# Per-head sums of squares as two products of the rounded 32-bit type

## The reference, cut to what matters

```python
def _rmsnorm(x, g):
    xf = x.astype(jnp.float32)
    r = lax.rsqrt(jnp.mean(xf * xf, axis=-1, keepdims=True) + EPS)
    return (xf * r).astype(x.dtype) * g

def _shared_kv(h, g, w_kv, f_bias, g_k):
    N, L, _ = h.shape
    k, v, f = jnp.split(_rmsnorm(h, g) @ w_kv, [D_ATTN, 2 * D_ATTN], axis=-1)
    k = _rmsnorm(k.reshape(N, L, N_HEADS, HEAD_DIM), g_k)
    ...
def _fox_layer(x, attend, g, w_in, g_q, w_out):
    q, z = jnp.split(_rmsnorm(x, g) @ w_in, 2, axis=-1)
    q = _rmsnorm(q.reshape(N, L, N_HEADS, HEAD_DIM), g_q)
    o = attend(q).reshape(N, L, D_ATTN)
    return x + (o * jax.nn.silu(z)) @ w_out
```

## Time and profile before

| what | us |
|---|---|
| median of 3 executions | 965.12 (964.96 to 965.85) |
| the profiled execution | 964.84 |
| its span, first to last instruction | 963.0 |
| PE busy | 931.7 (97% of the span) |
| DVE busy | 492.6 (51%) |
| ACT busy | 383.9 (40%) |
| POOL busy | 163.0 (17%) |
| granted TensorE clock | full (1.00) |

### The profile page before, as it was taken

One profiled execution on the slowest core, in us unless ns is written; L12 is line 12 of the kernel. 1 busy time (PEld: TensorE's weight loads), 2 busy tenths in 40 slices (PEclk: granted clock), 3 DMA queues, 4 the chain that ended last, 5 costly groups with the idle time before them and its releaser, 6 DMA issues.

```text
span 963.0 us, 23705 instructions
## 1 busy us (share of the span) xinstructions
PE 931.7 (97%) x8516; PEld 800.4 (83%) x8516; DVE 492.6 (51%) x1133; ACT 383.9 (40%) x728; POOL 163.0 (17%) x111
## 2 busy tenths in 40 slices
PE   4999999999999999999999999999999999999998
PEld 4999999999998997868778778688687787776898
DVE  5775555556345334463554554544545545535632
ACT  5333333322135443553543544535444445345210
POOL 2233333332030221102002012011020020000000
PEclk9999999999999999999999999999999999999999
DMA  7233322224343516889799799798996997987412
GB/s 235 67 88 87 87 70 83 81 72 118 127 153 115 174 57 201 284 292 351 239 367 332 238 385 302 264 380 257 329 348 233 371 328 240 383 297 254 142 44 99
DMA packets 133333, 206.41 MB, mean 214 GB/s; under 512 B 8847, under 2 KB 91456, under 8 KB 133170
## 3 DMA queue, kind: packets, MB, share of 16 engines
q1 hardware_dynamic: 121602, 198.35, 60.8%
q10 hardware_dynamic: 11168, 5.51, 2.1%
q0 software_dynamic: 528, 2.10, 0.8%
HBM read 195.29 MB, written 10.63 MB: 214 GB/s over the span
## 4 chain that ended last, share of the span: by engine, by line
PE 80%; DMA 6%; DVE 4%; ACT 3%; SPq 3%; issue 3%; ACTq 0%; DVEq 0%
PE psum L1221 41%; PE psum L1201 16%; PE psum L1270 9%; PE psum L1404 7%; DMA page_ring<-in_cache_k 4%; PE psum L1519 2%; ACT sample_scores L707 2%; SPq L375 2%; SPq L377 1%; DMA w_raw<-in_a_w_out 1%; PE psum L1447 1%; DMA residual<-in_x_prompt 1%; PE psum L1319 1%; PE psum L1427 1%; DMA page_ring<-in_cache_v 1%
## 5 line engine op out<-in xcount | busy, mean ns | idle before, releaser
L1221 PE MATMUL psum<-xn_high,w_high 128*128 128x256 f32 (+1 forms) x992 | 236.4, 317 | 2.6 <-DVE w_low L832 2.6
L1221 PE MATMUL psum<-xn_low,w_high 128*128 128x256 f32 (+1 forms) x992 | 215.8, 296 | 0.0
L1221 PE MATMUL psum<-xn_high,w_low 128*128 128x256 f32 (+1 forms) x992 | 215.6, 296 | 0.0
L1221 PEld LDWEIGHTS psum<-xn_high,w_high 128*128 128x128 f32 x992 | 163.1, 191 | 16.8 <-issue 13.3
L1221 PEld LDWEIGHTS psum<-xn_high,w_low 128*128 128x128 f32 x992 | 168.3, 190 | 0.0
L1221 PEld LDWEIGHTS psum<-xn_low,w_high 128*128 128x128 f32 x992 | 168.2, 190 | 0.0
L1201 PE MATMUL psum<-constants,page_ring 128*128 128x128 f32 x1024 | 136.9, 276 | 3.7 <-DMA page_ring<-in_cache_k 2.4
L1201 PEld LDWEIGHTS psum<-constants,page_ring 128*128 128x128 f32 x1024 | 114.0, 140 | 29.8 <-issue 27.6
L501 POOL TENSOR_TENSOR w_raw<-w_raw,gains 128x1024 f32<-128x1024 f32 x32 | 61.5, 1925 | 338.4 <-DMA w_raw<-in_b_w_in 217.6
L832 DVE TENSOR_TENSOR w_low<-w_raw,w_high 128x1024 fp32r<-128x1024 f32 x32 | 58.2, 1819 | 67.0 <-ACT w_high L565 67.0
L1009 DVE COPY k_turned_odd<-psum 128x512 f32<-128x512 f32 x64 | 44.1, 690 | 93.5 <-PE psum L1201 93.5
(11 more groups left out here) (236 smaller groups left out, 1467.8 us busy)
## 6 DMA issues: line engine op xcount, KB each, us to landing
page_ring<-in_cache_k SPq DMA_DIRECT2D x128, 512.0 KB, 5.8
page_ring<-in_cache_v SPq DMA_DIRECT2D x128, 512.0 KB, 5.2
w_raw<-in_a_w_in SPq DMA_DIRECT2D x30, 512.0 KB, 4.0
suffix<-suffix_scratch SPq DMA_DIRECT2D x32, 256.0 KB, 4.8
w_raw<-in_b_w_in SPq DMA_DIRECT2D x16, 512.0 KB, 6.8
w_raw<-in_kv_w SPq DMA_DIRECT2D x16, 512.0 KB, 6.2
w_raw<-in_a_w_out SPq DMA_DIRECT2D x4, 1024.0 KB, 5.1
f_broad<-f_scratch SPq DMA_DIRECT2D x8, 512.0 KB, 6.3
```

The source lines that it names most:

```text
L1221: mm = pe.matmul(PS[:, bank + h, 0:c.stop - c.start], w[:, k, :], x[:, k, c], start=(k == 0 and n == 0), stop=(k == KT - 1 and n == 2))
```

## The change

The squares are split like all other operands. DVE copies `SQ` to a rounded high part `SQH` (which lies in the last slab of the tile `gated_low`) and overwrites `SQ` with the rest, `SQL` (tile `squares_low`). PE multiplies both with a rounded copy of the ones matrix, `ONER`, and adds the two products in PSUM. In the query stage the sum moves from behind piece k = 2 to behind k = 3, and the split stands first in DVE's `query`, ahead of `low_b`. In the head stage the split stands at k = 6 behind the two gain instructions and ahead of the copy of T1; PE's sum stays behind the turns of k = 9.

```diff
         dve.wait_ge(s_fp, 1)
+        dve.tensor_copy(ONER[:, :], CT[:, C_ONESB:C_ONESB + P]).then_inc(s_one, 1)
...
+        def split_squares(high, done, n):
+
+            dve.tensor_copy(SQH, SQ[:, :]).then_inc(high, 1)
+            dve.wait_ge(high, n)
+            dve.tensor_tensor(SQL[:, :], SQ[:, :], SQH.bitcast(F32), ALU.subtract).then_inc(done, 1)
+
         def query(m, s):
+            dve.wait_ge(q_sq, m + 1)
+            split_squares(q_hi, q_sp, m + 1)
             low_b(m + 2, s)
...
                     dve.tensor_scalar(KN_T[:, SEQ:TOK], sa, gk, None, ALU.mult).then_inc(b_ddve, 1)
+                    dve.wait_ge(b_dact, 2 * i + 1)
+                    split_squares(b_hi, b_sp, i + 1)
                 turned1(KTS[k // 2 % 2][:, 4:8, c:c + PAGE],
...
+        def sum_squares():
+            for n, x in enumerate((SQH, SQL)):
+                pe.matmul(PS[:, OS, 0:NS], ONER[:, :], x[:, SEQ:TOK], start=(n == 0), stop=(n == 1))
+                mm = pe.matmul(PS[:, OP, :], ONER[:, :], x[:, 0:SEQ], start=(n == 0), stop=(n == 1))
+            return mm
...
-                if k == 2:
+                if k == 3:
                     if weights:
                         pe.wait_ge(s_fneg, 1)
-                    pe.wait_ge(q_sq, m)
+                        pe.wait_ge(s_one, 1)
+                    pe.wait_ge(q_sp, m)
...
         query(KT - 1, 1)
-        pe.wait_ge(q_sq, KT)
+        pe.wait_ge(q_sp, KT)
         pe.wait_ge(q_rr, KT - 1)
         q_sum()
...
-                    pe.wait_ge(b_dact, 2 * i + 1)
+                    pe.wait_ge(b_sp, i + 1)
```

More of the change, by code:

```diff
@@ L170, in build @@
     WFL = place("wf_low", [P, KT, H], F32R)
+    ONER = place("ones_blocks", [P, P], F32R, over=at["wf_high"])
+    SQL = place("squares_low", [P, TOK], F32R, over=at["squares"])
+    SQH = GL[:, KT - 1, :]
     PTAB = place("page_row", [1, NB * NPG], I32)
@@ L242, in build @@
     s_ck = sem("f_new_loaded")
+    s_one, q_hi, q_sp, b_hi, b_sp = (
+        sem("ones_ready"), sem("q_squares_high"), sem("q_squares_split"), sem("head_squares_high"),
+        sem("head_squares_split"))
     q_sq, q_ss, q_ln, q_rr, q_out = sem("q_squares"), sem("q_summed"), sem("q_ln"), sem("q_rsqrt"), sem("q_ready")
@@ L1315, in _ @@
         norm_turn(4, 1)
+        def sum_squares():
[3 more added lines that the diff above has]
+            return mm
         def q_sum():
-            pe.matmul(PS[:, OS, 0:NS], CT[:, C_ONESB:C_ONESB + P], SQ[:, SEQ:TOK], start=True, stop=True)
-            pe.matmul(PS[:, OP, :], CT[:, C_ONESB:C_ONESB + P], SQ[:, 0:SEQ], start=True, stop=True).then_inc(q_ss, 1)
+            sum_squares().then_inc(q_ss, 1)
         def query(m, s, weights=None):
@@ L1421, in heads @@
                 if k == 9:
-                    pe.wait_ge(b_dact, 2 * i + 1)
+                    pe.wait_ge(b_sp, i + 1)
                     pe.wait_ge(b_gf, i)
                     pe.wait_ge(b_sot, i)
-                    pe.matmul(PS[:, OS, 0:NS], CT[:, C_ONESB:C_ONESB + P], SQ[:, SEQ:TOK], start=True, stop=True)
-                    pe.matmul(PS[:, OP, :], CT[:, C_ONESB:C_ONESB + P], SQ[:, 0:SEQ], start=True, stop=True).then_inc(b_ss, 1)
+                    sum_squares().then_inc(b_ss, 1)
                 if k < 6:
```

## The result

| | before | after |
|---|---|---|
| median, us (lowest to highest, runs) | 965.04 (962.05 to 965.85, 4) | 978.15 (975.66 to 980.91, 4) |
| ratio, 95% interval | | 1.014 (1.0117 to 1.0163) |
| profiled execution: time, span | 964.84, 963.0 | 975.66, 973.8 |

The account below looks back on a forecast made before the run. PE's own stream was taken as the bound. 964.84 + 8.8 (eight head steps) + 0.7 (POOL in the first step) + 1.3 (query stage) = 975.6, stated as 975.4 us; range 970.5 to 980.5.

Parts of the forecast that it names:

- PE is the path, and DVE's order sets its waits: Head stage, k = 6: T1's copy waits behind DVE's split, stalling PE 1.5 us plus 0.05 in each of eight steps.
- The split: On DVE: a copy of 0.50 us and a subtraction of 0.76, with 0.03 between, 1.3 us (1.3 to 1.55).
- The sum on PE: Each of 16 sums of squares falls from 1.07 to 0.62 us, saving 0.45 (0.29 to 0.54).
- First head step: First head: the usual +1.1 us and +0.7 because the split waits for POOL's weight scaling; +1.8.
- Last stretch: Last gain to the end of the span, holding the eighth stall: +1.1 us.
- Query stage: From DVE's `f_raw` to the first head's gain: start, shorter periods, POOL and end together +1.3 us (-0.9 to +3.5).
- Collisions: Query stage: POOL's scaling meets the split in four queries, stalling PE 0.4, 0.8, 0.8 and 0.1 us, +2.1.
- Clean period: Query stage: one query without POOL in the way takes 7.1 us instead of 7.48, -0.38.
- PE doesn't need T1 early: Head stage: T1's copy has slack for the split, so only savings stay and the total is 962.5 us; 5%.
- waits for pages absorb it: Head stage: PE's waits for cached pages take up the stall, at most 4.6 us, total 971; 7%.
- POOL blocks more: POOL holds up the split in all queries and several head steps, total 980 us; 15%.
- 64 columns as dear as the full type: PE's sums: a rounded 64-column product costs as much as the full 32-bit one, 2.6 us more, total 978.0; 12%.

Follow-up runs that it names:

- x8_split_k7: Changed kernel with the head stage's split moved on DVE from k = 6 to the end of k = 7; 965.60 us, ratio 1.0005.
- x10_two_more_casts: Changed kernel with the old query stage and two more copies of the squares ahead of the heads' split; 988.48 us, ratio 1.0259.
- x4_pe_only: Changed kernel, but ACT writes rounded squares, no split, both products read them (low part left out), sum behind k = 2; 958.91 us, ratio 0.9940.
- x5_pe_only_cut: Changed kernel with ACT writing rounded squares, no split, low part left out, and sums cut 256 and 320 columns; 957.20 us, ratio 0.9902.
- x2_query_only: Changed kernel with the head stage of the kernel before, the query stage as changed; 966.81 us, ratio 1.0029.
- x6_small_pool: Changed kernel with POOL's scalings behind the fourth shrunk to eight elements, waits and signals kept; 976.11 us, ratio 1.0115.
- x3_late_split: Changed kernel with the head stage's split moved on DVE from k = 6 to the end of k = 8; 968.40 us, ratio 1.0049.
- x9_last_full: Changed kernel with the last query's sum in the full 32-bit type and unsplit; 977.73 us, ratio 1.0126.
- x7_best: Changed kernel with the old query stage, the heads' split at the end of k = 7 and their sums cut 256 and 320; 962.05 us, ratio 0.9969.

## Why the prediction was right, and where its sizes were off

- **PE is the path, and DVE's order sets its waits**: right. Eight waits at the named place. At the one worked out the fifth turn is 1.52 late against a forecast of 1.5, and 1.57 with the slower turn behind it against 1.55. `x8_split_k7` takes the wait away and 12.5 us with it; `x10_two_more_casts` lengthens it one for one.
- **The split**: 0.46 + 0.76, starts 0.50 apart, against 0.50 + 0.76. Right. The 0.36 us for the copy by the page's table (the Trainium skill, VectorE: DVE Perf Modes, errata cycle table), which the forecast had set aside, is 0.10 too short here. The same section says so itself: this row under-predicts, and the fixed part measures about 150 cycles, by which an estimate is (150 + 288) / 0.96 = 0.46 us, as in the trace.
- **The sum on PE**: mis-sized. I took 0.08 us for a rounded product of 64 columns; the sum came out at 0.68 instead of 0.62 and the saving at 0.40 instead of 0.45. Where the time goes is shown by `x4_pe_only` and `x5_pe_only_cut`: the even cut takes 0.53, so all that lies above it comes from the cut with 64 columns. In a head the stall was 1.57 for 1.55 and the saving 0.40 for 0.45, which makes up the 0.08 by which an ordinary step grew more than forecast (1.18 for 1.1).
- **First head step**: +2.3 for +1.8. Up to the piece behind the sum it went as forecast: the fifth turn is 2.11 late, 0.6 of it POOL's (PE waits 1.94 where the others are 1.36; forecast 0.7), and behind the sum PE is 1.77 late against the forecast's 1.8. The other 0.55 comes at the end of the step, at the value and key pages, which the forecast had put at nothing either way: PE waits 0.94 for a value page where it was 0.70 (the rows under the stages), and the turns of a key page 2 us later lose another 0.3. Why these pages come later stays open.
- **Last stretch**: +1.6 for +1.1. Its wait is longer than in an ordinary step (1.50 for 1.36), and PE waits 0.65 for a value page where it was 0.35. The stretch also moves by itself: in `x2_query_only`, with the heads of the kernel before, it takes 124.32 where that kernel took 124.69.
- **Query stage**: +2.8 for +1.3, and here the terms were wrong by different amounts. Collisions: 2.0 measured (`x6_small_pool`), 2.1 forecast; the agreement is luck, as the next point says. Clean period: 7.27 in the mean measured, 7.1 forecast; five times 0.17 is 0.85. Part of that is the sum's 0.06, since the chain to `q_out` runs through it. The 0.7 that is left is TensorE's clock behind the last query's wait: 6.94 in the changed kernel and 6.24 in two others with the same wait at a full clock, and 77.10 for 76.37 in two kernels that differ only in their heads. No term of the forecast held it.
- I had followed POOL's collisions as if they would fade (0.4, 0.8, 0.8, 0.1). They don't: the four periods are 0.4, 0.5, 0.5 and 0.5 longer than the clean one. POOL starts 3.9 to 4.0 us behind the end of `low_b`, which stands behind the split, so a delayed split delays the next scaling by as much, and the two meet at the same phase again, 7.8 us later each time.
- **Rivals.** *PE doesn't need T1 early* and *waits for pages absorb it* fell: the waits for pages are 4.2 us in all after 4.6. *POOL blocks more* fell in the heads for the place that the change chose, but `x3_late_split` shows how near it was: two pages later, four of eight splits are hit. *64 columns as dear as the full type* lies between: 0.68 is between my 0.62 and its 0.78.
- The net: heads +11.0 measured and +9.5 forecast, query stage +2.8 and +1.3, in all 13.8 and 10.8 (the stages' -2.9 at the start aside). The terms of the forecast itself add up to 975.6, and no term stands for the 0.2 by which it says 975.4. Of the 3.0 between, 0.6 lies in the ordinary head steps, 0.5 in the first, 0.4 in the last, 0.9 in the clean query periods and 0.7 in the clock.

## What to carry to other kernels

Before work goes to an engine that is half idle, look up what stands behind the place where it is put in that engine's queue, and which buffer the bound engine wants next: here the same two instructions cost 1.5 us per head behind page 6 and nothing that PE waited for behind page 7. Then look for long instructions of the neighbour that shares SBUF with it, at the new time of day, not the old one. And cut rounded products evenly: 256 and 320 columns took 0.27 us a set where 64 and 512 took 0.34. Cut evenly, the sum would save 0.54 us and not 0.40.

## What the hardware showed that I had not expected

- **DVE can be held for nearly a whole instruction of POOL.** A cast of 0.46 us took 1.90 and 1.97, and a subtraction of 0.76 took 2.33, under one scaling of 1.90, which itself took up to 2.14 in the changed kernel. The last is new beside the earlier trace rows: at 336.60 to 337.10 the cast, the scaling and the subtraction began within 0.5 us, the cast took its 0.46, and the two others ended later than each alone would have.
- **TensorE's clock can fall behind a single short wait.** The granted clock was 0.56 behind one of 2.09 us, 0.66 behind one of 2.87 and 0.75 and 0.68 behind one of 2.34, and 1.00 behind others of 2.09 and 2.34. The same wait of the same code came both ways, so its length alone does not decide it. At the last query that was worth 0.7 us; in `x10_two_more_casts` 1.5 in one step (69.17 for 67.69).
- **Code that nobody touched moves too.** The first 300 us varied by 6 us from one profiled execution to another. That is more than most of the effects that this study had to tell apart, which is why they are read from stages. In three of these executions (`x4_pe_only`, `x5_pe_only_cut`, `x9_last_full`) the clock falls once there as well, behind a wait of PE of 2.0 to 2.4 us near 252 us (0.66 from 252 to 257 in the first); it does not account for the whole spread, since `x7_best`, without it, has 306.3.
